# Output and down projections that end token by token, with filler transposes while TensorE waits

## What is computed

```
x = x + rms_norm(mix @ w_out[l], post_mix_norm[l])      # "out1"
h = rms_norm(x, pre_ffn_norm[l]); u = causal_dwconv(h @ w_up[l], ...)   # "up1"
y = (gelu(gate) * up) @ w_down[l]
x = x + rms_norm(y, post_ffn_norm[l])                   # "down1"
...                                                      # second block, from rmsnorm(x) @ w_in ("in2")
x = x + rmsnorm(m, norm_post_mix[i])                     # "out2"
h = rmsnorm(x, norm_pre_ffn[i])                          # "up2"
x = x + rmsnorm(conv_ffn(h, ...), norm_post_ffn[i])      # "down2", the output
```

## Time and profile before

| | us |
|---|---|
| median of 3 runs | 2549.88 |
| the three runs | 2558.95, 2549.88, 2548.95 |
| profiled execution, own time | 2559.84 |
| its span | 2557.6 |
| TensorE busy in it | 2511.5 (98%) |
| VectorE, ScalarE, GpSimd busy | 1653.1, 1333.7, 222.2 |

### The profile page before, as it was taken

The page is one execution under the profiler, slowest core; times in us unless marked ns, Lnnn a source line. Parts: engine busy times, 40 slices in busy tenths (PEclk is TensorE's granted clock), DMA queues, the critical chain, the costliest instruction groups (busy, mean ns, idle before and its releaser), DMA issues.

```text
span 2557.6 us, 40519 instructions
## 1 busy us (share of the span) xinstructions
PE 2511.5 (98%) x15344; PEld 2155.9 (84%) x15344; DVE 1653.1 (65%) x2014; ACT 1333.7 (52%) x1749; POOL 222.2 (9%) x94
## 2 busy tenths in 40 slices
PE   8999999999999999999999999999999999999997
PEld 8999877888888888887888888888788888888886
DVE  5665674677677775445485868775676676775444
ACT  5454564656556554444645455554555656554442
POOL 1000000022121211000000000000012131221000
PEclk9999999999999999999999999999999999999999
DMA  7865345566666666665655655546566666656664
GB/s 223 250 205 157 113 127 178 152 190 187 195 190 189 187 191 204 199 191 172 189 174 165 175 157 172 164 145 195 156 181 192 185 186 185 186 181 214 189 190 146
DMA packets 241791, 462.11 MB, mean 181 GB/s; under 512 B 14344, under 2 KB 23361, under 8 KB 241169
## 3 DMA queue, kind: packets, MB, share of 16 engines
q1 hardware_dynamic: 240001, 453.44, 58.7%
q0 software_dynamic: 1568, 7.10, 0.9%
q10 hardware_dynamic: 112, 0.03, 0.0%
HBM read 458.40 MB, written 2.12 MB: 180 GB/s over the span
## 4 chain that ended last, share of the span: by engine, by line
PE 98%; DVE 1%; ACT 1%; issue 0%; DMA 0%; SPq 0%; DVEq 0%; ACTq 0%
PE acc L231 13%; PE acc L233 13%; PE acc L232 13%; PE acc L251 13%; PE tp L251 13%; PE tp L253 7%; PE acc L253 7%; PE acc L828 3%; PE acc L830 2%; PE acc L831 2%; PE acc L1055 1%; PE acc L1057 1%; PE acc L1056 1%; PE tp L299 1%; PE tp L1535 1%; PE acc L836 1%
## 5 line engine op out<-in xcount | busy, mean ns | idle before, releaser
L218 DVE TENSOR_TENSOR wlo<-raw,whi 128x1024 fp32r<-128x1024 f32 x856 | 1070.8, 1258 | 761.6 <-ACT whi L213 759.8
L213 ACT ACTIVATE whi<-raw 128x1024 fp32r<-128x1024 f32 x856 | 903.3, 1059 | 1017.0 <-PE acc L233 467.5
L251 PE MATMUL acc<-ahl,whi 128*128 128x512 f32 x1408 | 495.1, 396 | 0.0
L251 PE MATMUL tp<-ahl,whi 128*128 128x512 f32 x1408 | 494.2, 395 | 0.0
L253 PE MATMUL acc<-ahl,wlo 128*128 128x256 f32 x1408 | 395.0, 281 | 0.0
L253 PE MATMUL tp<-ahl,wlo 128*128 128x256 f32 x1408 | 394.9, 280 | 0.0
L251 PEld LDWEIGHTS acc<-ahl,whi 128*128 128x128 f32 x1408 | 264.3, 188 | 62.3 <-issue 0.4
L251 PEld LDWEIGHTS tp<-ahl,whi 128*128 128x128 f32 x1408 | 263.9, 187 | 61.8
L231 PE MATMUL acc<-whi,ahl 128*128 128x512 f32 x768 | 305.7, 398 | 0.0
L233 PE MATMUL acc<-whi,ahl 128*128 128x512 f32 x768 | 299.9, 390 | 0.0
L232 PE MATMUL acc<-wlo,ahl 128*128 128x512 f32 x768 | 299.5, 390 | 0.0
(11 more groups left out here) (251 smaller groups left out, 2902.5 us busy)
## 6 DMA issues: line engine op xcount, KB each, us to landing
raw<-in_w_up_dram SPq DMA_DIRECT2D x176, 512.0 KB, 4.0
raw<-in_ffn_w_in_dram SPq DMA_DIRECT2D x176, 512.0 KB, 3.8
raw<-in_hgrn_w_in_dram SPq DMA_DIRECT2D x160, 512.0 KB, 3.6
raw<-in_w_in_dram SPq DMA_DIRECT2D x88, 512.0 KB, 3.7
raw<-in_w_down_dram SPq DMA_DIRECT2D x88, 512.0 KB, 3.9
raw<-in_ffn_w_out_dram SPq DMA_DIRECT2D x88, 512.0 KB, 3.7
raw<-in_w_out_dram SPq DMA_DIRECT2D x32, 512.0 KB, 3.7
raw<-in_hgrn_w_out_dram SPq DMA_DIRECT2D x32, 512.0 KB, 3.9
```

Of the source, the lines that this page charges most:

```text
L213: act.activation(whi[:, s, :], raw[:, s, :], ACT.Copy).then_inc(hi_done, 1)
L218: dve.tensor_tensor(wlo[:, s, :], raw[:, s, :], whi[:, s, :].bitcast(F32), ALU.subtract).then_inc(lo_done, 1)
L251: pe.matmul(o[:, ct % 2, :].rearrange("p (a t) -> p a t", a=2), whi[:, s, c], ahl[:, :, kt, :], start=(kt == 0), stop=False, skip_group_ch ...
```

## The change

In out1, down1, out2 and down2 the last four chunks of the last group are multiplied by `last_products`: all four for token 0, then all four for token 1. The slots are released in the second pass. Sum and scaling of the first three groups' squares are taken ahead (`rest_dve`). `last_act` squares a token of the last group into the other accumulator and takes its root with the rest as bias, and VectorE works by token (`last_dve`): reciprocal, additions, ybuf, and between them the splits of two of the next phase's chunks, of which the third moves behind the first `alo`. `pre_pe_by_token` transposes the first two quarters by token. `keep_busy` puts transposes of the identity where TensorE waits: 26 before the parameters' rows, 18 behind the first transposes of in1, and 12 and 7 in each of the three crossings. The products of the down projections are no longer a loop of two rounds on TensorE. The output leaves as one transfer for token 0 and four for token 1.

The diff, without the same edits for out2 and the calls' arguments:

```diff
@@ -287,6 +287,12 @@
 LEAD = 3
+def keep_busy(pe, bank, n):
+    for j in range(n):
+        pe.transpose(bank, ident[:, :], ident[:, :])
 TAIL_HI, TAIL_LO = 7, 8
...
@@ -298,6 +304,19 @@
     mm.then_inc(sem("pre_turned"), 1)
+def pre_pe_by_token(pe, ph, src, ready):
+    for t in range(NT):
+        for q in range(2):
+            if t:
+                keep_busy(pe, tp[1][:, 0, P:2 * P], 7 if q else 12)
+            ready(pe, q, t)
+            for k in range(4):
+                c = (4 * q + k) * P
+                mm = pe.transpose(tp[q][:, k, t * P:(t + 1) * P], src[:, t, c:c + P], ident[:, :])
+            if t == NT - 1:
+                mm.then_inc(sem("pre_turned"), 1)
...
@@ -320,7 +339,9 @@
-    for q in {0: (0, 1), 2: (2,), 4: (3,)}.get(c, ()):
+    if c == 0:
+        pre_pe_by_token(pe, ph, src, ready)
+    for q in {2: (2,), 4: (3,)}.get(c, ()):
         pre_pe(pe, ph, q, src, ready)
...
@@ -331,13 +352,14 @@
     if c == 3:
-        source(0)
-        source(1)
         pre_dve(dve, ph, 0, gain)
-        source(2)
+        s_lo(dve, ph, 0, 0, 2)
+        for t in range(NT):
+            source(2, t)
         pre_dve(dve, ph, 1, gain)
     if c == 4:
-        source(3)
+        for t in range(NT):
+            source(3, t)
     if c == 5:
...
@@ -367,24 +389,86 @@
-def back_pe(pe, ph, xhi, xlo, nch, ready=None, ready_count=None, last_count=None, src=None, src_ready=None):
-    def body(i, first):
+def last_products(pe, ph, k, n, xhi, xlo, kts):
+    out = acc[(gb[ph] + NG - 1) % 2]
+    for t in range(NT):
+        for j in range(RING):
+            if t == 0:
+                pe.wait_ge(lo_done, n + j + 1)
+            s = (n + j) % RING
+            for kk in range(CK):
+                kt, c = kts[j] + kk, slice(kk * GC, (kk + 1) * GC)
+                xh, xl = xhi[:, kt, t * P:(t + 1) * P], xlo[:, kt, t * P:(t + 1) * P]
+                pe.matmul(out[:, t, :], xh, whi[:, s, c], start=False, stop=False)
+                pe.matmul(out[:, t, :], xh, wlo[:, s, c], start=False, stop=False)
+                mm = pe.matmul(out[:, t, :], xl, whi[:, s, c], start=False, stop=(j == RING - 1 and kk == CK - 1))
+            if t:
+                mm.then_inc(chunk_used, 1)
+        if t == 0:
+            mm.then_inc(sem("token0"), 1)
+def last_act(act, ph, k, t, end):
+    a, other = acc[(gb[ph] + NG - 1) % 2], acc[(gb[ph] + NG) % 2]
+    if t == 0:
+        act.wait_ge(sem("token0"), k + 1)
+    else:
+        act.wait_ge(chunk_used, end)
+    act.activation(other[:, t, :], a[:, t, :], ACT.Square, accum_out=psq[:, k, t, NG - 1:NG])\
+       .then_inc(sem("last_sq"), 1)
+    act.wait_ge(sem("last_sq"), NT * k + t + 1)
+    act.wait_ge(sem("rest"), 2 * k + 2)
+    act.activation(prs[:, k, t:t + 1], psq[:, k, t, NG - 1:NG], ACT.Sqrt, scale=1.0 / D,
+                   bias=prs[:, k, t:t + 1]).then_inc(sem("post_root"), 1)
+def rest_dve(dve, ph, k):
+    dve.wait_ge(group_free, gb[ph] + NG - 1)
+    dve.tensor_reduce(prs[:, k, :], psq[:, k, :, 0:NG - 1], AX.X, ALU.add).then_inc(sem("rest"), 1)
+    dve.wait_ge(sem("rest"), 2 * k + 1)
+    dve.tensor_scalar(prs[:, k, :], prs[:, k, :], 1.0 / D, EPS, ALU.mult, ALU.add).then_inc(sem("rest"), 1)
+def last_y(dve, ph, k, t, gain_row):
+    dve.wait_ge(sem(f"{ph}_gain"), 16)
+    dve.wait_ge(sem("last_sq"), NT * k + t + 1)
+    c = slice((NG - 1) * GC, NG * GC)
+    m = dve.tensor_tensor(ybuf[:, t, c], acc[(gb[ph] + NG - 1) % 2][:, t, :], gain_row[:, c], ALU.mult)
+    m.then_inc(group_free if t else sem(f"{ph}_y"), 1)
+def unroot_dve(dve, ph, k, t):
+    dve.wait_ge(sem("post_root"), NT * k + t + 1)
+    dve.reciprocal(prs[:, k, t:t + 1], prs[:, k, t:t + 1]).then_inc(sem("post_rs"), 1)
+    dve.wait_ge(sem("post_rs"), NT * k + t + 1)
+def last_dve(dve, ph, k, gain_row, nxt):
+    add = add_rows(dve, ph, k)
+    unroot_dve(dve, ph, k, 0)
+    add(0, 0)
+    last_y(dve, ph, k, 0, gain_row)
+    s_lo(dve, nxt, 0, 0, 0)
+    add(1, 0)
+    s_lo(dve, nxt, 0, 0, 1)
+    unroot_dve(dve, ph, k, 1)
+    add(0, 1)
+    last_y(dve, ph, k, 1, gain_row)
+    add(1, 1)
+def back_pe(pe, ph, k, nch, ready):
+    pe.wait_ge(ready, FG)
+    for i in range(2):
         for c in range(2 * nch):
             if c % nch == 0:
                 group(pe, gb[ph] + c // nch + 2 * i)
-            if first:
-                lead_pe(pe, ph, c, src, src_ready)
-            if last_count and CK * c == 4 * (FG - 1):
-                pe.wait_ge(ready, last_count)
-            products(pe, cb[ph] + c + i * (2 * nch), c % RING, acc[(gb[ph] + c // nch) % 2],
-                     xhi, xlo, CK * (c % nch), CK * nch, ph if first and c < nch else None)
-    if src is None:
-        pe.wait_ge(ready, ready_count)
-        with pe.Fori(0, 2) as i:
-            body(i, False)
-    else:
-        body(0, True)
-        body(1, False)
+            if CK * c == 4 * (FG - 1) and not i:
+                pe.wait_ge(ready, FG + 1)
+            if not i or c < 2 * nch - RING:
+                products(pe, cb[ph] + c + i * (2 * nch), c % RING, acc[(gb[ph] + c // nch) % 2],
+                         hhi, hlo, CK * (c % nch), CK * nch)
+    last_products(pe, ph, k, cb[ph] + 4 * nch - RING, hhi, hlo, [CK * (nch - RING + j) for j in range(RING)])
...
@@ -407,55 +491,57 @@
-def back_act(act, ph, k, nch, last=False):
+def back_act(act, ph, k, nch, nxt):
     for i in range(2):
-        for c in range(LEAD if i else TAIL_HI, 2 * nch):
+        for c in range(LEAD if i else TAIL_HI, 2 * nch + (0 if i else LEAD)):
             s_hi(act, ph, i, 2 * nch, c)
             if c == nch + 3:
                 back_group_act(act, ph, k, i, 0)
-        if not (i and last):
-            for c in range(2 * nch, 2 * nch + LEAD):
-                s_hi(act, ph, i, 2 * nch, c)
-        back_group_act(act, ph, k, i, 1)
-    act.wait_ge(sem(f"{ph}_post"), 2)
-    act.activation(prs[:, k, :], prs[:, k, :], ACT.Sqrt).then_inc(sem(f"{ph}_post"), 1)
-def back_dve(dve, ph, k, nch, gain_row, last=False):
+        if not i:
+            back_group_act(act, ph, k, i, 1)
+    last_act(act, ph, k, 0, cb[ph] + 4 * nch)
+    if nxt:
+        for c in range(LEAD):
+            s_hi(act, nxt, 0, 0, c)
+    last_act(act, ph, k, 1, cb[ph] + 4 * nch)
+def back_dve(dve, ph, k, nch, gain_row, nxt):
     for i in range(2):
-        for c in range(LEAD if i else TAIL_LO, 2 * nch):
+        for c in range(LEAD if i else TAIL_LO, 2 * nch + (0 if i else LEAD)):
             s_lo(dve, ph, i, 2 * nch, c)
             if c == nch + 3:
                 back_group_dve(dve, ph, i, 0, nch, gain_row)
-        if not (i and last):
-            for c in range(2 * nch, 2 * nch + LEAD):
-                s_lo(dve, ph, i, 2 * nch, c)
-        back_group_dve(dve, ph, i, 1, nch, gain_row)
-    post_root_dve(dve, ph, k)
-def post_root_dve(dve, ph, k):
-    dve.wait_ge(group_free, gb[ph] + NG)
-    dve.tensor_reduce(prs[:, k, :], psq[:, k, :, :], AX.X, ALU.add).then_inc(sem(f"{ph}_post"), 1)
-    dve.wait_ge(sem(f"{ph}_post"), 1)
-    dve.tensor_scalar(prs[:, k, :], prs[:, k, :], 1.0 / D, EPS, ALU.mult, ALU.add)\
-       .then_inc(sem(f"{ph}_post"), 1)
-    dve.wait_ge(sem(f"{ph}_post"), 3)
-    dve.reciprocal(prs[:, k, :], prs[:, k, :]).then_inc(sem(f"{ph}_post"), 1)
-    dve.wait_ge(sem(f"{ph}_post"), 4)
+            if i and c == nch + 7:
+                rest_dve(dve, ph, k)
+        if not i:
+            back_group_dve(dve, ph, i, 1, nch, gain_row)
+    if nxt:
+        last_dve(dve, ph, k, gain_row, nxt)
+    else:
+        for t in range(NT):
+            unroot_dve(dve, ph, k, t)
+            add_rows(dve, ph, k)(0, t)
+            last_y(dve, ph, k, t, gain_row)
+            for q in range(1, NG):
+                add_rows(dve, ph, k)(q, t)
 def add_rows(dve, ph, k):
-    def add(q):
+    def add(q, t):
         c = slice(q * GC, (q + 1) * GC)
-        for t in range(NT):
-            dve.scalar_tensor_tensor(out=x[:, t, c], in0=ybuf[:, t, c], scalar=prs[:, k, t:t + 1],
-                                     in1=x[:, t, c], op0=ALU.mult, op1=ALU.add)\
-               .then_inc(sem(f"{ph}_x"), 1)
+        if q == NG - 1 and t == 0:
+            dve.wait_ge(sem(f"{ph}_y"), NT * (NG - 1) + 1)
+        if q == NG - 1 and t == 1:
+            dve.wait_ge(group_free, gb[ph] + NG)
+        dve.scalar_tensor_tensor(out=x[:, t, c], in0=ybuf[:, t, c], scalar=prs[:, k, t:t + 1],
+                                 in1=x[:, t, c], op0=ALU.mult, op1=ALU.add)\
+           .then_inc(sem(f"{ph}_x"), 1)
     return add
 def x_ready(ph):
-    def wait(e, q):
-        e.wait_ge(sem(f"{ph}_x"), 2 * q + 2)
+    def wait(e, q, t=None):
+        e.wait_ge(sem(f"{ph}_x"), 2 * q + 2 if t is None else 2 * t + q + 1)
     return wait
...
@@ -473,12 +559,12 @@
         for c in range(BODY):
-            if first and c == 0:
-                pe.wait_ge(group_free, gb[ph])
-            elif c % CPG == 0 and not first:
+            if c % CPG == 0 and not first:
                 group(pe, gb[ph] + c // CPG + i * 2)
```

(27 more changed lines are left out.)

39 lines of the change are left out of this document (18 added, 21 removed).

## The result

The kernel after takes 2535.77 us, the median of seven runs (2525.02 to 2543.67); the kernel before, run seven times on the same chip, 2558.95 (2548.95 to 2559.7). The ratio is 0.9912, with a 95% interval of 0.9884 to 0.9940: faster by 22.4 us between the means and 23.2 between the medians, where the prediction's sum was 23.2.

What follows compares the result with a forecast made beforehand. TensorE was taken as the bound, busy 2511.5 of 2557.6 us, with 46.1 left to win beside lower-clock stretches. Terms 5.2 + 4.4 + 5.7 + 5.2 + 2.7 = 23.2 us off the median gave 2526.7, range 2519 to 2540.

Steps and rivals of the forecast that it cites:

- Crossings of out1 and out2: Where out1 and out2 end: first next product at E (last product's end) + 4.25, not E + 8.6; 4.4 us each.
- Clock behind the crossings: Full clock for the first products after a crossing: 0.8 us saved behind out1, 1.1 behind down1, nothing behind out2.
- down1: Crossing from down1 to in2: first product at E + 4.9 instead of 9.5, 4.6 us, with clock 5.7 saved.
- The end: After down2: span ends at E + 8.0 instead of 13.2, limited by the output's transfers; 5.2 us saved.
- The start: Fillings raise the clock early: first product 11.0 against 11.76, 0.75 saved, first 22 products 2.0 faster; sum 2.7 us.
- What could be late next: Splits of the last and next phase's chunks, and weight loads behind them, might come late; taken as 0.
- Case 5: Written-out down projections run at half the pace of loops: 239 us more, 2766 us; chance 0.03.
- The level: Runs lie on two levels 10 us apart; the 23.2 us were taken off before's median of three runs, giving 2526.7.
- Case 1: All terms come as reckoned: 2526.7 us, with 4 us to either side; chance 0.80.

Runs made afterwards that it cites:

- the repeat: The kernel after run again with no edit, six runs beside other kernels on the same chip: median 2526.91 us, ratio 0.9906 to before.

## Why the prediction was right, step by step

The measured 2535.77 is within the range, and the terms of the crossings, the end and the start came out by the mechanisms that were forecast. Two things were luck or nearly so: that the terms left out in the first stage cancel in the profile of the kernel after, and that the level, which was taken wrongly, was covered by the range.

**Crossings of out1 and out2.** E + 4.29 for E + 4.25. Token 0's part was reckoned within 0.4 us (its first addition ends at E - 3.4 for E - 3.6, VectorE's second wlo split at E + 0.1, where the queue's end was put at E + 0.5), and the steps behind token 1's root within 0.1. What the chain's order alone does and what the fillings do was not told apart in the sum; it is 3.5 and 0.9 (fillings on the old order).

**Clock behind the crossings.** 0.8 was reckoned at out1, 0.92 measured. For out2 nothing was counted, because before's clock was up again by its first product. That stands against before. But in the new order without fillings the clock would fall there too, at a cost of 1.45. The forecast didn't name what the fillings hold there.

**down1.** The first product came at E + 4.52, not 4.9. VectorE and ScalarE in the kernel after (E is 1184.41):

```profile
1179.71 1.28 ACT L422 ACT_TABLE_LOAD   x1
1181.01 0.29 ACT L422 ACTIVATE prs<-psq,prs 128x1 f32<-128x1 f32 x1
...
1184.60 1.22 DVE L218 TENSOR_TENSOR wlo<-raw,whi 128x1024 fp32r<-128x1024 f32 x1
...
1185.74 0.15 DVE L443 RECIPROCAL prs<-prs 128x1 f32<-128x1 f32 x1
```

The mechanism is the one forecast: the table load stands under token 1's products, and VectorE's second wlo split, not token 1's root (1185.17, 0.29), comes last before the reciprocal. The reciprocal started at E + 1.33, where the split was forecast to end at E + 1.75: the queue is 0.4 shorter than the sum of its rounded steps. Token 0's root starts 0.02 behind the end of the table load, as in before (0.01). By the Trainium skill, ScalarE: Activation LUTs, section What ACT_TABLE_LOAD costs, a drain of about 1.38 us would lie on top; again no row shows one. The 1.1 for the clock came out as 1.0. The row has 1.92, but in2's stage took 592.7 or 593.6 in the profiles of the changed kernels, against 594.62, and the 0.9 between the two isn't the clock's: with a granted clock of 1.00 in both it is spread over the products of the stage, and which of the two it is doesn't follow the crossing.

**The end.** 7.63 for 8.0, 5.56 less for 5.2. The bound is the transfers, as was reckoned; they were 5.4 us long and their first issue came at E + 0.48 and not at 0.7.

**The start.** First product at 11.01 and products 0.12 apart, as reckoned; the second group of transposes stands 2.76 earlier than in before, for the 2.7 of the sum. But what was gained at 14 us isn't all kept: E of out1 lies 0.5 (without cross fillings), 1.1 (the repeat), 2.9 (the kernel after) or 4.6 (with out1's waits filled and the scores halved) earlier than in before. The forecast took the time between as unchanged. It isn't. By the table of parts, the first stage's 2.16 in the kernel after is 1.65 up to the scores, for the 2.0 reckoned; then 1.5 are lost, since the clock fell behind the scores as it didn't in before; then 2.0 are won, since it fell once and not twice at out1's waits, and the second wait was shorter. In the repeat the three are 2.0, -3.1 and 1.5, and the stage gives 0.5. That 2.16 is so near 2.0 is luck.

**What could be late next** was put at 0, rightly: no wait for a split is in TensorE's list, and the weights follow. **Case 5** (written-out down projections) can be closed too: up1 and down1 took 729.94 us in the kernel after and 730.04 in the kernel before with fillings alone, where the loops are still in place. The instruction queue moved 86 packets instead of 77, at no cost.

**The level** was the weak step. "I see nothing in its waits that the change would touch" was right, and the sum was rightly taken from executions of the same level. But the forecast took the lower level for the median, from three runs of before; in all seven the median of before is on the upper level, 2558.95, and so is that of the kernel after. Case 1's own 4 us would not have covered 2535.77; the range did, as it had been widened for the levels. The forecast of a difference (23.2, measured 22.4 to 23.2 and by levels 22.4 to 23.3) was much better than that of a time (2526.7, measured 2535.77, in the repeat 2526.91).

## What to carry to other kernels

Where a phase ends in a reduction over what it has just computed, let the last few chunks run by token, long enough that the first token's whole chain fits under the second token's products; two chunks were too few here, four were enough. Fill the waits that remain on TensorE with transposes that end before the data comes: the filling costs nothing, and keeps the clock where waits of 1.2 and 0.6 us, close together, dropped it at two of three places. Look at the end for the moment at which the first transfer can leave, not for the last computation.

## What the runs showed of the hardware

- A stream of matmuls has two paces at the same granted clock and busy share: 0.3466 and 0.3533 us a pair, 9 us over an up phase. It changed only where the stream was interrupted by transposes. It fits the levels on which the runs of both kernels lie (one profile of the upper level), and its cause is open.
- TensorE can lose its clock while it is busy: behind 32 matmuls of 15 columns in a row it was 0.50 to 0.83 over 4 us in ten profiles of the twelve in which they stand together, at 1.5 or 3.1 us each; not in before and not with twice the fillings. 16 and 16 with products between them held 1.00, in the one profile taken.
- Transposes of the identity bring the clock up and hold it: at the start 26 in 5.07 us, and the next eight in 1.09 instead of 1.97; in the crossings 1.00 with them, against 0.63 and 0.57 behind two of three without.
